# Weight slots in two halves with a gap, in a trunk kernel of 15,360 matmuls of 128x288: where each moving row lies against its weight tile

## The reference, cut to what matters

```
def swiglu(h, w_gate, w_up, w_down):
    return (jax.nn.silu(h @ w_gate) * (h @ w_up)) @ w_down
...
    h = rmsnorm(x, p['norm_pre'][0])
    x = x + 0.5 * rmsnorm(swiglu(h, p['w_ffn_gate'][0], p['w_ffn_up'][0], p['w_ffn_down'][0]), p['norm_post'][0])
    h = rmsnorm(x, p['norm_pre'][1])
    m, h_last, new_conv, S_fin = mixer(h, st_h, st_conv, st_gla, reset_first, p)
    x = x + rmsnorm(m, p['norm_post'][1])
    h = rmsnorm(x, p['norm_pre'][2])
    x = x + 0.5 * rmsnorm(swiglu(h, p['w_ffn_gate'][1], p['w_ffn_up'][1], p['w_ffn_down'][1]), p['norm_post'][2])
```

## Time and profile before

| what | value |
|---|---|
| time, median of 3 runs | 2160.32 us (2160.12 to 2160.43) |
| time of the profiled execution | 2159.84 us |
| its span | 2157.8 us |
| granted TensorE clock, mean | 1.0 |
| TensorE matmul busy | 2150.2 us, 17197 matmuls |
| DVE, ACT, POOL busy | 1440.1, 1292.4, 704.9 us |

### The profile page before, as it was taken

One profiled execution on the slowest core, in us unless ns is written; L12 is line 12 of the kernel. 1 busy time (PEld: TensorE's weight loads), 2 busy tenths in 40 slices (PEclk: granted clock), 3 DMA queues, 4 the chain that ended last, 5 costly groups with the idle time before them and its releaser, 6 DMA issues.

```text
span 2157.8 us, 41190 instructions
## 1 busy us (share of the span) xinstructions
PE 2150.2 (100%) x17197; PEld 2126.5 (99%) x17197; DVE 1440.1 (67%) x1902; ACT 1292.4 (60%) x1989; POOL 704.9 (33%) x708
## 2 busy tenths in 40 slices
PE   9999999999999999999999999999999999999999
PEld 9999999999999999999999999999999999999998
DVE  7555857678986658845584558577699867576454
ACT  7534657648785556653564356576578765575444
POOL 3112512525554225511240124024265533152111
PEclk9999999999999999999999999999999999999999
DMA  7555555445554455555555555554455545555553
GB/s 255 166 164 159 167 177 154 147 142 172 166 157 139 147 183 161 166 166 164 164 163 164 168 165 162 172 158 145 141 183 157 157 138 152 182 161 163 163 169 126
DMA packets 100551, 350.98 MB, mean 163 GB/s; under 512 B 11408, under 2 KB 12304, under 8 KB 100368
## 3 DMA queue, kind: packets, MB, share of 16 engines
q1 hardware_dynamic: 99936, 347.68, 52.7%
q10 hardware_dynamic: 432, 0.68, 0.1%
HBM read 343.45 MB, written 4.87 MB: 161 GB/s over the span
## 4 chain that ended last, share of the span: by engine, by line
PE 96%; DVE 1%; POOL 1%; issue 1%; DMA 0%; ACT 0%; SPq 0%; DVEq 0%; POOLq 0%; ACTq 0%
PE psD L513 92%; PE psM L606 1%; POOL ssum L1646 1%; PE psM L513 0%; DVE val L1502 0%; PE psM L647 0%; DVE wl L1177 0%; PE psM L719 0%; PE psM L682 0%; POOL hidl L1847 0%; DMA raw<-in_w_gu 0%; PE psS L533 0%; PE psM L726 0%; PE psD L499 0%; PE psM L586 0%
## 5 line engine op out<-in xcount | busy, mean ns | idle before, releaser
L513 PE MATMUL psD<-hh,wh 128*128 128x288 f32 x3664 | 1093.4, 298 | 0.4 <-DVE hl L1245 0.4
L513 PE MATMUL psD<-hl,wh 128*128 128x288 f32 x3664 | 1080.9, 295 | 0.0
L513 PE MATMUL psD<-hh,wl 128*128 128x288 f32 x3664 | 1077.4, 294 | 0.0
L1177 DVE TENSOR_TENSOR wl<-raw,wh 128x1024 fp32r<-128x1024 f32 (+2 forms) x656 | 823.2, 1256 | 111.0 <-ACT wh L833 110.4
L833 ACT ACTIVATE wh<-raw 128x1024 fp32r<-128x1024 f32 (+2 forms) x656 | 671.6, 1026 | 95.2 <-DMA raw<-in_w_gu 46.8
L513 PEld LDWEIGHTS psD<-hh,wh 128*128 128x128 f32 x3664 | 686.7, 187 | 6.8 <-issue 3.7
L513 PEld LDWEIGHTS psD<-hh,wl 128*128 128x128 f32 x3664 | 690.0, 188 | 0.0
L513 PEld LDWEIGHTS psD<-hl,wh 128*128 128x128 f32 x3664 | 688.0, 188 | 1.7
L1847 POOL TENSOR_TENSOR hidl<-hid,hidh 128x288 fp32r<-128x288 f32 x176 | 214.1, 1217 | 904.1 <-ACT hidh L1121 904.1
L513 PE MATMUL psD<-hidh,wh 128*128 128x288 f32 x1408 | 417.6, 297 | 0.4 <-POOL hidl L1847 0.4
L513 PE MATMUL psD<-hidl,wh 128*128 128x288 f32 x1408 | 415.4, 295 | 0.0
(11 more groups left out here) (256 smaller groups left out, 1570.7 us busy)
## 6 DMA issues: line engine op xcount, KB each, us to landing
raw<-in_w_gu SPq DMA_DIRECT2D x351, 512.0 KB, 3.5
raw<-in_w_d SPq DMA_DIRECT2D x128, 448.0 KB, 3.3
raw<-in_w_in SPq DMA_DIRECT2D x80, 512.0 KB, 3.6
raw<-in_w_d SPq DMA_DIRECT2D x64, 512.0 KB, 3.6
raw<-in_w_out SPq DMA_DIRECT2D x32, 512.0 KB, 3.6
x<-in_xT SPq DMA_DIRECT2D x8, 288.0 KB, 6.9
gates<-in_w_ax SPq DMA_DIRECT2D x4, 512.0 KB, 4.5
S<-in_st_gla SPq DMA_DIRECT2D x4, 512.0 KB, 4.5
```

Of the source, the lines that this page charges most:

```text
L513: mm = e.matmul(out, w[:, kt * P:(kt + 1) * P], t[:, kt, :], start=(kt == 0 and part == 0), stop=(kt == KT - 1 and part == 2))
L1177: e.tensor_tensor(wl[u % RING][:, part], raw[u % RING][:, part], wh[u % RING][:, part].bitcast(F32), ALU.subtract).then_inc(lo_ready, 1)
```

## The change

It lays the ring of weight slots out anew, and the order of the moving rows with it:

- A slot is two halves of 2048 bytes with 128 bytes between them, and the next slot begins 4224 bytes (`PITCH`) behind it, the gap again between. The ring begins 112 bytes (`LEAD`) on.
- In every second unit the two halves are swapped. The host lays the weights out in this way, gap included, so one DMA of 4224 bytes a partition (3712 for seven tiles) fills a slot.
- In units of eight tiles ACT and DVE go over the two halves and leave the gap out. In units of seven tiles they go over 928 floats, the gap with them, where it was 896.
- Rows of `hh` and `hl` are placed in the order 0, 4, 1, 5, 2, 6, 3, 7, rows of `hidh` and `hidl` as before. For the down projections the halves are the even and the odd tiles, for the others the first four and the last four.
- By these sizes a moving row lies 144 bytes off its own tile, modulo 256, for each kt, each slot, and for high and low weights alike. While the last matmul of a tile runs, the weights of the next tile are loaded. Where that tile is in the other half, the running row is mostly 16 bytes off it: at 2 of 24 matmuls in a full unit of the other projections, at 8 of 24 or 6 of 21 in a down projection.
- To make room, `wg2` holds one layer, and the other layer's weights are loaded in its place in layer 1. TensorE has a wait for that load.

```diff
+HALF = D // 2
+GAP = 32
+PITCH = D + GAP
+LEAD = 28
...
+def tile_in_slot(u, kt):
+    second, at = (kt % 2, kt // 2) if SOURCES[u][0].startswith("w_d") else (kt // (DT // 2), kt % (DT // 2))
+    first = span(u).start
+    return (HALF + GAP if second ^ (u % 2) else first) + at * P
+
+
+def span(u):
+    missing = (DT - depth(u)) * P
+    return slice(missing, PITCH) if u % 2 else slice(0, PITCH - missing)
...
-        hh.append(sb(f"hh{g}", [P, DT, T], F32R))
-        hl.append(sb(f"hl{g}", [P, DT, T], F32R))
+        for part, name in ((hh, "hh"), (hl, "hl")):
+            t = sb(f"{name}{g}", [P, DT, T], F32R)
+            part.append([t[:, 2 * (k % (DT // 2)) + k // (DT // 2), :] for k in range(DT)])
...
-    wh = [sb(f"wh{s}", [P, D], F32R) for s in range(RING)]
-    raw_at = cursor[0]
-    raw = [sb(f"raw{s}", [P, D]) for s in range(RING)]
-    cursor[0] = raw_at
-    wl = [sb(f"wl{s}", [P, D], F32R) for s in range(RING)]
...
+    def slot_of(t, s):
+        return t[:, LEAD + s * PITCH:LEAD + (s + 1) * PITCH + GAP]
+
+    def halves(slot):
+        return slot.rearrange("p (h c) -> p h c", h=2)[:, :, 0:HALF]
+
+    def parts_of(u, slot):
+        if u == 0:
+            return slot[:, HALF + GAP:PITCH]
+        return halves(slot) if depth(u) == DT else slot[:, span(u)]
+
+    wh = [slot_of(ring, s) for s in range(RING)]
+    wl = [slot_of(ring, RING + s) for s in range(RING)]
+    raw = [slot_of(raw_ring, RING + s) for s in range(RING)]
...
-                    e.dma_start(raw[u % RING][:, 0:depth(u) * P], a[name][at, :, :]).then_inc(raw_landed[u % RING], 16)
+                    e.dma_start(raw[u % RING][:, span(u)], a[name][at, :, :]).then_inc(raw_landed[u % RING], 16)
...
+                    if i == 2:
+                        e.wait_ge(logit_done, i)
+                        e.dma_start(wg2[:, :], a["w_g2"][:, s.l, :]).then_inc(wg2_landed, 16)
...
+                at = tile_in_slot(u, kt)
                 for part, (w, t) in enumerate([(w_h, xh), (w_h, xl), (w_l, xh)]):
-                    mm = e.matmul(out, w[:, kt * P:(kt + 1) * P], t[:, kt, :],
+                    mm = e.matmul(out, w[:, at:at + P], t[kt],
                                   start=(kt == 0 and part == 0), stop=(kt == KT - 1 and part == 2))
...
-                e.activation(wh[u % RING][:, part], raw[u % RING][:, part], ACT.Copy).then_inc(hi_ready, 1)
+                w_h, w = parts_of(u, wh[u % RING]), parts_of(u, raw[u % RING])
+                e.activation(w_h, w, ACT.Copy).then_inc(hi_ready, 1)
...
-                e.tensor_tensor(wl[u % RING][:, part], raw[u % RING][:, part], wh[u % RING][:, part].bitcast(F32),
-                                ALU.subtract).then_inc(lo_ready, 1)
+                w_l, w, w_h = (parts_of(u, t[u % RING]) for t in (wl, raw, wh))
+                e.tensor_tensor(w_l, w, w_h.bitcast(F32), ALU.subtract).then_inc(lo_ready, 1)
```

More of the change, by code:

```diff
@@ L498, in unit @@
                     for t in (xh, xl):
[L499 removed]
+                        e.matmul(out, w_h[:, tile_in_slot(u, kt):tile_in_slot(u, kt) + P], t[kt], start=(kt == 0 and t is xh), stop=False)
                 e.wait_ge(lo_ready, u + 1)
                 for kt in range(KT):
[L502 removed]
+                    mm = e.matmul(out, w_l[:, tile_in_slot(u, kt):tile_in_slot(u, kt) + P], xh[kt], start=False, stop=(kt == KT - 1))
                 mm.then_inc(unit_done, 1)
@@ L608, in recurrence @@
                 if slot == 6:
+                    e.wait_ge(wg2_landed, 16 * (s.l + 1))
                     e.wait_ge(gd_ready, i + 1)
                     for pr in range(PR):
-                        mm = e.matmul(psM[:, 2 + pr, 0:T], wg2[:, s.l, pr * P:(pr + 1) * P], gd[g][:, :], start=True, stop=True)
+                        mm = e.matmul(psM[:, 2 + pr, 0:T], wg2[:, pr * P:(pr + 1) * P], gd[g][:, :], start=True, stop=True)
                     mm.then_inc(logit_done, 1)
@@ L1525, in _ @@
         lo(5)
[L1526 removed]
+        e.wait_ge(const_landed, 16 * 5)
         newton(rstd[0])
@@ L1875, in layouts, with tiles @@
     f = np.float32
-    def units(w):
+    def tiles(w):
         *lead, K, N = w.shape
@@ L1880, in units @@
         k = len(lead)
-        return w.transpose(*range(k), k + 2, k + 1, k, k + 3).reshape(*lead, N // P, P, K)
+        return w.transpose(*range(k), k + 2, k + 1, k, k + 3).reshape(-1, P, K // P, P)
+    def units(w, down=False):
+        n, _, K, _ = w.shape
+        order = [[*range(0, K, 2)], [*range(1, K, 2)]] if down else [[*range(DT // 2)], [*range(DT // 2, K)]]
+        first, second = (w[:, :, o].reshape(n, P, -1) for o in order)
+        gap = np.zeros((n, P, GAP), f)
+        rows = np.stack([np.concatenate([first, gap, second], axis=2), np.concatenate([second, gap, first], axis=2)], axis=1)
+        return rows[np.arange(n), np.arange(n) % 2]
     def vec(v):
@@ L1914, in layouts @@
         "w_ax": gates.reshape(L, P, LT, 2 * P),
-        "w_out": units(w_out).reshape(-1, P, D),
+        "w_out": units(tiles(w_out)),
         "par": par.reshape(P, L * NPAR),
@@ L1924, in layouts @@
         rows = slice(STARTS[c] * P, (STARTS[c] + n) * P)
-        out[f"w_d{c}"] = units(w_ffn_down[:, :, rows, :]).reshape(-1, P, n * P)
+        out[f"w_d{c}"] = units(tiles(w_ffn_down[:, :, rows, :]), down=True)
     return out
```

61 lines of the change are left out of this document (31 added, 30 removed).

## The result

The changed kernel takes 2133.05 us (median of four runs, 2132.81 to 2133.73) against 2160.22 for the one before (2159.84 to 2160.43): ratio 0.9875, 95% interval 0.9858 to 0.9892. It is faster by 27 us, where 93 were forecast.

The account below looks back on a forecast made before the run. The prediction took dense TensorE as the bound: unit matmuls at 133.3 ns, 13.3 over their columns. From 2159.84 it took 99.8 for layout and added 7 for DVE, 2067.0, stated as 2067 us; 8-in-10 range 1998 to 2162.

Parts of the forecast that it names:

- What bounds the kernel: TensorE: a matmul under way for 2150.2 of 2157.8 us, waits 3.0 us, so time is matmul count by pace.
- A fixed cost of swapping weights is 2.3 ns at most, the other 11.0 appear only where a row is read at a column a cycle: Unit matmuls: 13.3 ns over 120 split into 2.3, from L550's plain float32, and 11.0 that a layout might remove.
- The second rival: Addresses don't matter: excess belongs to a row read at a column a cycle; 2160 us within 2, chance 0.18.
- 15,360 x 6.5 ns = 99.8 us: Gain from the new layout of rows and tiles, 6.5 ns on each unit matmul, chosen between 0 and 11.0.
- The two hints read from rows: Signs of varying pace: down units hold 123 starts against 122 in 16 us; distances after L537 are 135 and 130 ns.
- Distances of 144 and 16: Row-to-tile offsets modulo 256: 144 was to avoid over half the read meetings; 15% of matmuls, 2208, get 16.
- The new distance is worse: Third rival: rows stopped repeatedly beside tiles, 1.7 ns on every unit matmul, 26 us slower, 2186 us; chance 0.15.
- DVE gives back 7 us: In the mixers DVE is full, so faster TensorE waits there: 5.9 us nearly all lost, 7 with bursts elsewhere.
- Waits growing to 10 us: Sign of being right: TensorE's waits grow from 3 us to about 10, for DVE's `wl` in two stretches.
- Longer rows: Seven-tile units: splits over 928 floats for 896 add 40 ns on DVE, 34 on ACT; no cost while there's room.
- `wg2`: The reload for layer 1 lands with 12 us to spare; TensorE's new wait costs nothing.
- Two ports: The Trainium skill's independent SBUF ports for loading and reading: the layout would change nothing, 2160 us; chance 0.18.

Follow-up runs that it names:

- b4: TensorE alone, one thing changed per stretch (format, banks, partitions, widths) at three row-to-tile distances: at 288 columns, distance 0, fp32r 131.6 ns, bfloat16 122.5, plain float32 242.5.
- b2: TensorE alone: 16 row starts by 16 tile starts in 16-byte steps, also narrower tiles and other unit orders; 130.0 to 134.9 ns over the map.
- b5: TensorE alone: the changed kernel's order and its down units' alternating order at 16 ring starts each; 131.12 and 131.10 ns at 112 bytes, alternating 130.00 at 192.
- b3: TensorE alone: unit order of the kernel before, without halves, 16 row starts by 16 ring starts; 131.08 ns at best, 133.33 unshifted, 134.46 at worst.
- v4: Kernel before with only the ring begun 96 bytes on, no halves or gaps; 2167.63 us, ratio 1.0036.
- v1: Kernel before with only the ring begun 112 bytes on, no halves, gaps, reordered rows or `wg2` reload; 2132.55 us, ratio 0.9875.
- b6: TensorE alone: five unit orders, each run behind 24 different matmuls; alternating tiles with the ring at 192 settle at 130.00 ns behind 23, 132.21 behind one.
- v9: v8 with only the tile `ones` moved 128 bytes further modulo 256; 2122.71 us, ratio 0.9826.
- b7: TensorE alone: two orders behind a pair placed like the kernel's token sums, its tile at 16 places; three places throw the alternating order to 132.2 ns.
- v8: Changed kernel with tiles alternating between halves in every unit, ring 192 bytes on, tiles laid out as read; 2127.82 us, ratio 0.9851.
- b1: TensorE alone, one row and one tile repeated at distances up to 496 bytes, also other row widths and unit orders; 130.8 to 133.4 ns over distances.

## Why the prediction was wrong

**What bounds the kernel** was right: TensorE dense, waits of 3.8 us, all of the gain in the distances of the units' matmuls.

**"A fixed cost of swapping weights is 2.3 ns at most, the other 11.0 appear only where a row is read at a column a cycle"**: the number holds for plain float32 (242.5 in b4). bfloat16 is at 122.5 with rows of 288 columns in 120 ns, a column a cycle as well, so the other 11.0 belong to fp32r and not to that rate alone. The step that failed is the next: to read those 11.0 as meetings of row read and tile read, and so as something that a layout takes away. Of the 13.3 ns some 10 stay in the best layout of b2 to b5 (130.0). They stay with a quarter of the tile read, with rows of 240 to 512 columns (24 to 48 cycles, with no proportion to the columns), in other banks and on half the partitions. L550 has no such excess because plain float32 hasn't any, at any of three distances, not because it misses the tile. The second rival was right for three quarters of the excess, which no layout tried touches, though its reason, a row at a column a cycle, falls with bfloat16. A slip on the way cost nothing: 0.8 x 128 is 102 and not 107.

**The term 15,360 x 6.5 ns = 99.8 us** measured 15,360 x 1.8 = 28 us (2.2 ns where nothing disturbs a unit). It was set between bounds of 0 and 11.0 by the failed picture; the lower bound was the nearer. The sign came out right for another reason: 133.33 is among the slow paces of b3, whose mean over 256 starts is 132.4, so that most moves gain something. That this one hit 131.1, near the best, was luck: nothing in the picture tells a start of 112 bytes from one of 96, where v4 loses. The two hints read from rows were real: the pace isn't one number (123 for 122, and the earlier trace rows), though no run says whether addresses or what went ahead made these differences. Their size, 0.6 to 5 ns between places, holds the size of the effect. The term should have been taken from them (2 to 3 ns, some 40 us), not from the far end of the interval.

**Distances of 144 and 16.** The change's halves, which give nearly all matmuls one distance, didn't matter: v1 has other distances and the same 131.12 in units of eight tiles, 131.4 for 131.1 in those of seven. That the prediction took the distance as the quantity was wrong twice: b2 has 130.0 to 132.8 for the change's distance at different row starts, and b6 has different paces for the same addresses.

**The new distance is worse** (third rival): not at 112, but v4 shows that the risk was real, at 96, 16 bytes away. With the change's halves b5 has 132.5 there, a smaller gain and no loss.

**DVE gives back 7 us**: mis-sized. DVE is as full as it was; this stretch of after does the work of 1660 to 1680 in the earlier trace rows:

```profile
1640.00:1660.00 20.00, 20.00 (x149) 19.68 (x148) 19.73 (x37) 17.54 (x27) 5.78 (x10) 1.00 0.48 154
```

The two output projections of the first group (26.49 and 26.52 us from first start to the next stage's) last 26.48 and 26.54, where their 192 matmuls at 2.2 ns less would have saved 0.4 each. The two stages of input projection beside them save 0.7 where 1.06 was due. That is some 1.5 us in all, since the pace rose by 1.7% and not by 5.

**Waits growing to 10 us**: 3.8, for the same reason. **Longer rows, `wg2`, two-half accesses cost nothing**: right, and v1 without them has the same time. 40 and 34 ns were foretold for the longer splits, 27 and 27 measured; full splits are 7 ns longer, 4 us of DVE in its slack. The start off a multiple of 32 bytes isn't the reason: v4, with slots on multiples of 32, has 1292 ns as v1 has with slots 16 bytes past one, and before and v9 have 1287.

**Two ports.** The Trainium skill, "TensorE: Matmul & The Clock Gate" (Part 2, Step-by-step), has loading and reading independent, from which the prediction made its second rival. For bfloat16 and plain float32 b4 agrees: none of the three distances tried changes anything. For fp32r the start of the weights alone changes the pace of the matmuls, v1 against v4, 35 us for 16 bytes; whether the two reads get into each other's way there, or something else does it, no run shows.

**What stays open.** What the 24 cycles are that fp32r keeps in every layout tried. And what inside the chip has the rhythm: a period of 256 bytes in the addresses and a few levels, many of them 1.1 ns (2.7 cycles) apart, are what the runs show. A version with shifted rows as well wasn't tried in the whole kernel, since the operands fill their regions to the byte.

## What to carry to other kernels

A bound taken from another form of an instruction (plain float32 for fp32r) is not a bound that a layout can reach: measure the loop alone, one thing changed at a time, before a term of 100 us is built on it; where two ends of an unknown lie far apart, the variation that the trace itself shows is the better guide to size than the middle. In a dense stream of fp32r matmuls with a weight load each, start addresses modulo 256 bytes moved the pace from 133.3 ns down to 130.0 and up to 134.5 by itself, and a whole kernel from 2160 us down to 2123 and up to 2168, and no rule for them came out of these runs: try layouts in a kernel of TensorE alone, behind several different matmuls, and choose one whose pace is the same behind all. Then look in the whole kernel at the pace of single units, ahead of and behind side work, since an average hides two rhythms.

## What was unexpected of the hardware

- The same matmuls at the same addresses settle into one of two paces, 130.00 and 132.21 ns (133.33 and 134.44 in another layout), and keep it for hundreds of matmuls; one or two other matmuls ahead of them can decide which (b6, b7, v8 and v9).
- 16 bytes in the start of the weights decide between 2132.55 and 2167.63 us (v1, v4).
- A matmul with a weight load takes 2.5 ns over its columns for bfloat16 (122.5 at 288, 215.8 at 512) and for a pass of plain float32 (122.5 at 144, 242.5 at 288), at each of three distances, and 10 to 15 ns at 288 columns of fp32r (b2, b4).
- With a float32 tile of 128 columns loaded for each, fp32r matmuls of 64, 192 and 224 columns all go at 111.6 to 111.7 ns (b1).
- Tiles of 32 columns under rows of 288 swap hardly cheaper than tiles of 128 (26.8 and 28.1 cycles over), although a load of 32 lasts 108 ns and one of 128 lasts 188 (b2).
